# Twelve modulation units moved from the weight slots into row buffers, ahead of tile 0's projection back

## What is computed

```python
# first block, per tile of 128 tokens
proj = rms_norm(x) @ w_in                       # S5 input, q, k, v, two gates
y_s5 = s5_mixer(u) @ w_s5_branch                # state space model, GELU, GLU
y_attn = sliding_window_attention(q, k, v) @ w_attn_branch
h = x + (g_s5 * y_s5 + g_attn * y_attn) @ w_out # "projection back"
h = h + peer_mixer(rms_norm(h))                 # 8 heads x 16 experts per token
# second block
mod = silu(c) @ w_mod + b_mod                   # c is ONE row; w_mod is 1024 x 6144
sh1, sc1, gt1, sh2, sc2, gt2 = split(mod, 6)
# norm * (1 + sc) + sh, sparse attention and a short convolution, @ w_out, then PEER again
```

## Time and profile before

| | |
|---|---|
| three runs | 3271.86, 3277.43, 3278.6 us; median 3277.43 |
| the profiled execution | 3271.78 us, span 3270.2 us |
| mean granted TensorE clock | 0.847 |
| TensorE busy | 75% of the span |
| VectorE busy | 71% |
| ScalarE / POOL busy | 41% / 34% |
| bytes moved by DMA | 1295.01 MB, mean 396 GB/s |
| queue of the gathers / of SP's loads | 81.2% / 17.1% of the 16 engines' span |

### The profile page before, as it was taken

The page is one execution under the profiler, slowest core; times in us unless marked ns, Lnnn a source line. Parts: engine busy times, 40 slices in busy tenths (PEclk is TensorE's granted clock), DMA queues, the critical chain, the costliest instruction groups (busy, mean ns, idle before and its releaser), DMA issues.

```text
span 3270.2 us, 40578 instructions
## 1 busy us (share of the span) xinstructions
PE 2448.9 (75%) x14052; PEld 1033.6 (32%) x14052; DVE 2319.4 (71%) x5500; ACT 1330.7 (41%) x3602; POOL 1125.9 (34%) x1038
## 2 busy tenths in 40 slices
PE   8968779786797777878788869778877656555555
PEld 3432333223332233335442426423334211111111
DVE  8448783878839787485875685888866777777644
ACT  2114432444424444243583343468734433333222
POOL 0012342324413243232343333444433444443432
PEclk9979879897898988989898879878888876777877
DMA  9899999999999999999999999999999999999997
GB/s 254 316 362 415 413 402 385 407 410 414 411 386 417 408 418 410 384 391 390 376 386 394 402 409 398 399 409 418 386 414 406 407 418 419 418 418 410 420 420 319
DMA packets 214057, 1295.01 MB, mean 396 GB/s; under 512 B 26934, under 2 KB 30294, under 8 KB 82776
## 3 DMA queue, kind: packets, MB, share of 16 engines
q0 software_dynamic: 148320, 1076.50, 81.2%
q1 hardware_dynamic: 64860, 213.81, 17.1%
q10 hardware_dynamic: 672, 2.12, 0.2%
HBM read 1289.62 MB, written 2.71 MB: 395 GB/s over the span
## 4 chain that ended last, share of the span: by engine, by line
PE 36%; DMA 24%; DVE 22%; issue 9%; ACT 4%; POOL 3%; SPq 0%; POOLq 0%; ACTq 0%; DVEq 0%
PE ps L1722 12%; DMA ring<-in_k_uv,idx 12%; PE ps L1802 10%; DVE ring L415 9%; DMA ring<-in_k_vu,idx 8%; PE ps L2096 5%; DMA wsl<-in_k_wu 4%; POOL ring L2400 3%; PE ps L2106 2%; DVE big L470 2%; ACT L1249 1%; PE ps L1977 1%; PE ps L1779 1%; DMA wsl<-in_k_wmod 1%; ACT diag L1249 1%
## 5 line engine op out<-in xcount | busy, mean ns | idle before, releaser
L1722 PE MATMUL ps<-ring,diag 64*64 64x512 f32 x8192 | 1261.6, 741 | 480.3 <-ACT diag L1249 450.6
L415 DVE CUSTOM_DVE_ANT_0 ring<-ring,xn 128x1024 f32<-128x1024 f32 x1024 | 1238.8, 1220 | 442.6 <-DMA ring<-in_k_vu,idx 233.6
L2400 POOL DMA_INDIRECT ring<-in_k_vu,idx x514 | 558.6, 1087 | 1135.2 <-DVE aw L415 653.2
L2400 POOL DMA_INDIRECT ring<-in_k_uv,idx x510 | 561.2, 1100 | 934.7 <-DVE aw L415 650.2
L1722 PEld LDWEIGHTS ps<-ring,diag 64*64 64x64 f32 x8192 | 310.0, 158 | 1244.5 <-ACT diag L1249 726.8
L1249 ACT ACTIVATE aw<-aw 128x2 f32<-128x2 f32 x512 | 103.6, 202 | 998.1 <-DVE aw L415 996.8
L1249 ACT ACTIVATE diag<-gid,aw 128x64 f32<-128x64 f32 x1024 | 312.3, 342 | 330.6 <-PE ps L1722 314.9
L1249 ACT ACT_TABLE_LOAD x339 | 434.9, 1283 | 22.4 <-issue 10.4
L1802 PE MATMUL ps<-wsl,xT 128*128 128x512 f32 x896 | 423.7, 619 | 26.3 <-DMA wsl<-in_k_wu 22.3
L1249 ACT ACTIVATE gid<-ident,gate 128x64 f32<-128x64 f32 x1024 | 292.4, 332 | 0.0
L1802 PEld LDWEIGHTS ps<-wsl,xT 128*128 128x128 f32 x896 | 167.2, 196 | 282.8 <-issue 234.6
(11 more groups left out here) (264 smaller groups left out, 2129.2 us busy)
## 6 DMA issues: line engine op xcount, KB each, us to landing
wsl<-in_k_wu SPq DMA_DIRECT2D x342, 512.0 KB, 9.2
wsl<-in_k_wmod SPq DMA_DIRECT2D x40, 512.0 KB, 6.7
ring<-in_k_vu,idx POOLq DMA_INDIRECT x514
ring<-in_k_uv,idx POOLq DMA_INDIRECT x510
ring<-in_k_wmod SPq DMA_DIRECT2D x8, 512.0 KB, 9.5
wsl<-in_k_wu SPq DMA_DIRECT2D x8, 280.0 KB, 13.9
hres<-in_x SPq DMA_DIRECT2D x4, 512.0 KB, 5.5
pers<-L1d POOLq DMA_DIRECT2D x8, 256.0 KB, 15.3
```

The lines of the kernel that those rows point to most:

```text
L415: V(v.tensor_tensor_reduce(u_row(s), u_row(s), xn[:, n % 3, :], 1.0, 0.0, ALU.mult, ALU.add, aw[:, b, k:k + 1]), ("dot", s))
L1722: r = t.matmul(PA[half][64 * q:64 * q + 64, :], diag[64 * half:64 * half + 64, s % (2 * PAIR), :], v_row(s)[64 * half:64 * half + 64, 512 ...
L2400: Q(p.indirect_dma_start(out=both_rows(s), out_offset=None, in_=tab, in_offset=bass.IndirectOffsetOnAxis(ap=idx[:, n % 2, k:k + 1], axis=0 ...
```

## The change

Modulation units 28 to 39 (rows 7, 8 and 9) leave the list of slot units. They are loaded into twelve ring places instead: 28 to 35 into the eight places of units 0 to 7, and 36 to 39 into ring rows 6 to 9. SP issues the twelve in one go just before the first unit of tile 0's projection back, after it has waited for TensorE's modulation unit 7 and for tile 0's attention. On POOL the second gather now waits for modulation unit 35 and the third for unit 39, since their rows hold those units. In `mod(u)` these units are read from the ring.

```diff
+        again = {28 + e: w for e, w in enumerate(early)}
+        again.update({36 + e: carve(rflat, 6144 + 1024 * e, 2, 512)[0] for e in range(4)})
+        in_rows = {**dict(enumerate(early)), **again}
...
-                             ((0, "wq"), range(16, 24)), ((0, "sk"), range(24, 28)), ((1, "win"), range(28, 48))):
+                             ((0, "wq"), range(16, 24)), ((0, "sk"), range(24, 28)), ((1, "win"), range(40, 48))):
...
-                if u < len(early):
-                    w, used = early[u], []
+                if u in in_rows:
+                    w, used = in_rows[u], []
                     T.wait_ge("early", u)
...
+                if s == 1:
+                    G.wait_ge("mod_mm", 35)
+                if s == 2:
+                    G.wait_ge("mod_mm", 39)
...
+                if (n, name, b, u) == (0, "wout", 0, 0):
+                    Y.wait_ge("mod_mm", 7)
+                    Y.wait_ge("a_pv", 0, 1)
+                    for e, w in again.items():
                         src = A["k_wmod"][131072 * e:131072 * e + 131072].rearrange("(p k n) -> p k n", p=128, n=512)
                         Q(s.dma_start(w, src), "early%d" % e, ("early", e))
```

More of the change, by code:

```diff
@@ L2438, in extra @@
                     for e, w in enumerate(early):
+                        src = A["k_wmod"][131072 * e:131072 * e + 131072].rearrange("(p k n) -> p k n", p=128, n=512)
+                        Q(s.dma_start(w, src), "early%d" % e, ("early", e))
+                if (n, name, b, u) == (0, "wout", 0, 0):
+                    Y.wait_ge("mod_mm", 7)
+                    Y.wait_ge("a_pv", 0, 1)
+                    for e, w in again.items():
                         src = A["k_wmod"][131072 * e:131072 * e + 131072].rearrange("(p k n) -> p k n", p=128, n=512)
```

## The result

The changed kernel takes 3286.89 us in the median of 6 runs (3281.86 to 3290.6), the kernel before 3275.07 (6 runs, 3271.36 to 3278.6). The ratio is 1.0032 with a 95% interval of 1.0017 to 1.0047: slower by 10.5 us, 6 to 15. The forecast was 3286, within 3273 to 3297. That the measured 3286.89 lies within 1 us of it is in part luck: the forecast was +9 us on a median of 3277.4, and the kernel before came out at 3275.07 here. The profiled execution took 3281.86 us, its span is 3280.2, 10.0 more than before.

A forecast was written before the change was run, and what follows sets the result against it. DMA and VectorE were both taken to bind at 240 to 320 us. Delay 13.3 + 2.0 = 15.3 us, less what comes back, left 8.5 to 9.8: +9 on 3277.4, forecast 3286, range 3273 to 3297.

The forecast's parts named there:

- Twelve loads in front of the projection back: SP queue before tile 0's projection back: 15.2 us of transfers make its first unit land at 165.4, 13.3 us late.
- The clock: TensorE after idling before the projection back: lower granted clock costs 2.0 us, bounds 0 to 14.
- What comes back, by engines: Last four modulation units need no load, so VectorE's xT of tile 1 regains 5.5 us: 9.8 us late.
- What comes back, by bytes: DMA up to the first gather: 15.3 late, less 8.8 of lead, plus 2 for restart: 8.5 us late.
- the lead: By the first gather, units up to 46 have landed instead of 39 or 40: 7 units, 8.8 us.
- the restart: DMA runs dry before the first gather; starting again costs some 2 us.
- Which balance counts: From 240 to 320 us VectorE and DMA both bind, so the later balance counts: between 8.5 and 9.8, +9 us.
- The gathers' waits: POOL's second gather waits 0; the third is 0.5 us late behind two gathers, so cost 0.
- Full return of the bytes: Rival at tile 1's DMA-bound stage: the full 15.2 us comes off, net 0 to +3, up to 6; chance 0.27.
- a gain from shorter waits beside gathers: Rival: seven units fewer beside gathers return 26.5 us to tile 1, net -11 us, 3266; chance 0.10.
- The further loss: Rival: TensorE's low clock covers the whole projection, 14 instead of 2 us; total +12 to +20, 3289 to 3297; chance 0.10.

The follow-up runs named there:

- cost_only: Kernel before plus the twelve loads in front of tile 0's projection back, nothing taken off the slots: 3292.18 us against 3274.41, ratio 1.0058.
- eight: Changed kernel with only units 28 to 35 moved, 36 to 39 staying in slots, third gather without new wait: 3284.55 us against 3273.38, ratio 1.0031.
- behind_four: Changed kernel with the twelve loads behind the fourth unit of the projection back instead of before the first: 3283.78 us against 3272.90, ratio 1.0032.
- waits_only: Kernel before with only the second and third gathers' new waits, on modulation units 35 and 39: 3275.95 us against 3274.41, ratio 1.0011.
- return_only: Changed kernel without the twelve loads, slots relieved, modulation rows 7 to 9 wrong: 3272.16 us against 3274.41, ratio 0.9990.
- seven_early: Kernel before with units 28 to 32 moved behind the second GLU unit, 33 and 34 into modulation row 2: 3277.48 us against 3273.38, ratio 1.0010.
- spread12: Changed kernel with the twelve loads spread, one behind every second unit from the projection back to the queries: 3280.74 us against 3274.41, ratio 1.0021.
- four_early: Kernel before with only units 28 to 31 moved, behind the second GLU unit: 3270.46 us against 3273.38, ratio 0.9986; repeated, ratio 1.0004.

## Why the prediction was right

- *Twelve loads in front of the projection back.* Forecast start 165.4, measured 165.26 and in cost_only 164.62. eight and behind_four put the wait where a queue in order puts it, and the twelve landed in order, the last at 163.93. This is shown for loads on SP's queue; no run issues them from another engine, so what another queue would do is open.
- *The clock.* Forecast 2.0 us, from one row. The stage took 15.88 us after, 15.65 in cost_only, 16.60 in eight, and 13.97 in the kernel before and those that start it on time: 1.7 to 2.6. The later query projection had 15.78 instead of 16.62, so the indices are 14.3 late and not 15.3. That 0.8 need not be the change's: the same stage took from 13.97 to 16.68 us in these kernels, 13.97 in waits_only, which up to there is the kernel before. Against that execution (first indices at 207.9) the changed kernel's are 17.7 us late. So the size of the delay at the first indices is right to some 3 us, and that it came out so near is in part luck.
- *What comes back, by engines.* Forecast 5.5, measured 4.7 (14.3 late at the indices, 9.6 at xT). The last row of the modulation lost its waits for units, as forecast.
- *What comes back, by bytes.* Two sizes, the lead and the restart, were off. From 149.5 to 213 us the kernel before moves 10.5 us at 404 GB/s, 40 at 304 and 13 at 408, 21.7 MB. From 149.5 to 228 the changed one moves 15.5 us at 410, 35 at 333, 15 at 311 and 13 at 124, 24.3 MB. So 2.6 MB or 4.9 units more, not 7: in bytes under way the kernel before had come to unit 41 at 213 (the last one landed by then, at 212.38, is unit 38; I had 39 or 40). At 415 GB/s that is 6.2 us of the 15 by which the window is longer, 8.8 late. After it the gathers alone did not fill the DMA at once, 394 GB/s from 228 to 253 against 414: 1.2 us, where I had put 2. That gives 10.0 late by bytes. Ahead of 149.5 us the changed kernel had moved some 0.5 MB more, 1.1 us, 0.2 MB of it in the 0.6 us to spare that the forecast counted; so from the start of the span it is 8.9 (328 against 339 GB/s up to 335 us), forecast 8.5.
- *Which balance counts.* I took both as binding, VectorE by its 75.98 of 80 us. In these traces only the DMA's rate stays the same (415 GB/s), so the bytes decide. Here the two lie within 1 us (8.9 and 9.6), and no harm came of it; in eight they lie 2.5 us apart (6.4 and 8.9), and the total of 10 is nearer to the bytes.
- *The gathers' waits.* Forecast 0.5 us for the third. It was 1.7 (3.01 after the second, 1.27 in the kernel before). TensorE ran row 9 at the lower granted clock with a gap (226.08 to 230.70). Its cost in the total is within -1 to 9 us by waits_only, where the gather is held 1.06 us and not 2.04; that it is small is argued, from the 0.6 us there.
- *The rivals.* Full return of the bytes and a gain from shorter waits beside gathers are ruled out by return_only and seven_early. The further loss (low clock through the whole stage) did not come.
- *Open.* Why the later part of a run adds or takes some microseconds. It does so in most kernels here, and in spread12 and eight the totals lie 6 and 4 us above what the index times show at 316 us. By bytes, with the query projection put back, eight's gap is 1 us and spread12's 5, where the interval just reaches down to it.

## What to carry to other kernels

A load moved ahead in a busy queue costs its full transfer time to whatever stands behind it and is wanted next, even where windows show unused DMA time a little later; look for the hole at the load's new place (four_early found one and delayed nothing), and at who is queued behind. What it gives back is bounded by what may run in its old place: here seven slots, which were full soon, so more than half of the relieved 15.2 us became idle DMA time ahead of the first gather (13 us at 124 GB/s instead of 408 is 9 us). Work out both in bytes per window before you move a load. And when two traces are compared, compare a stage that the change does not touch first: here one such stage differed by 2.65 us.

## What the runs showed of the hardware

SP's issues took longer behind the twelve loads. The twelve themselves went out at 0.55 us each. The seven projection units behind them took 1.08 us each in the median; the same instruction takes 0.33 in the kernel before. In cost_only it is 1.08 too. That the number of loads under way is the reason is my reading; no run varies it alone. First the changed kernel's row from 148 to 165 us, then that of before from 143.5 to 155 (minimum, median and maximum in ns).

```profile
L2425 SPq DMA_DIRECT2D wsl<-in_k_wu x7: 1072/1077/2297, 149.3 to 157.3; - x7
```

```profile
L2418 SPq DMA_DIRECT2D wsl<-in_k_wu x8: 327/328/558, 144.5 to 154.1; - x8
```

The same 32 matmuls of the query projection took 16.62 us in one profiled execution and 13.97 in others whose work up to there is the same in kind, with a mean granted clock of 0.84 over the stage in the first and 1.00 in return_only and waits_only. TensorE had idled about 3 us and then 1 us ahead of it in each, and the length of that idle time does not tell them apart: 3.24 us before the 16.62, 3.16 and 2.80 before the 13.97 of return_only and waits_only. At the first indices the difference is about 3 us, a quarter of this change's whole effect, and a single profile would have given it to any change.
